# A kernel of two transformer blocks: the last attention pair's softmax rows over three PSUM banks, the low-rank weights loaded with the constants, and two more gate units in the first recurrence pair

## What is computed

```python
for g, (window, dilation) in enumerate(DILATED_GROUPS):
    num, den, mx = dilated_group_attention(...)
m_all = jnp.max(jnp.stack(maxes), axis=0)
wts = [jnp.exp(mx - m_all) for mx in maxes]
num_tot = sum(w[..., None] * n for w, n in zip(wts, nums))
den_tot = sum(w * d for w, d in zip(wts, dens))
o_attn = (num_tot / den_tot[..., None]).reshape(B, S, ATTN_WIDTH)
...
w_log = -jax.nn.softplus(-(rwkv_w0[l] + jnp.tanh(w_low) @ rwkv_w_up[l])) - 0.5
decay = jnp.exp(-jnp.exp(w_log))
a = jax.nn.sigmoid(rwkv_a0[l] + a_low @ rwkv_a_up[l])
...
y = rwkv7_scan(r4, decay.reshape(hs), k4, v4, -kk, kk * a.reshape(hs))
...
merged = jax.nn.sigmoid(g_attn) * y_attn + jax.nn.sigmoid(g_rwkv) * y_rwkv
```

## Time and profile before

| | |
|---|---|
| median of 3 runs | 2949.07 us (2947.56 to 2949.91) |
| the profiled execution | 2949.86 us, of which the traced span is 2948.1 us |
| mean granted PE clock | 0.961 |
| PE busy | 2738.0 us, 93% of the span |
| DVE busy | 1342.5 us, 46% |
| ACT busy, POOL busy | 815.2 and 818.1 us, 28% each |

### The profile page before, as it was taken

One profiled execution on the slowest core, in us unless ns is written; L12 is line 12 of the kernel. 1 busy time (PEld: TensorE's weight loads), 2 busy tenths in 40 slices (PEclk: granted clock), 3 DMA queues, 4 the chain that ended last, 5 costly groups with the idle time before them and its releaser, 6 DMA issues.

```text
span 2948.1 us, 43284 instructions
## 1 busy us (share of the span) xinstructions
PE 2738.0 (93%) x17944; PEld 2184.3 (74%) x17944; DVE 1342.5 (46%) x2316; ACT 815.2 (28%) x1584; POOL 818.1 (28%) x453
## 2 busy tenths in 40 slices
PE   6999999987979999999898999999998989999896
PEld 5787878775757667576677888788886877777675
DVE  4225252527647465474541433544444023677703
ACT  2444444443113131220212211211113013344432
POOL 2222222212112121220244132222332445333253
PEclk9999999998989999999999999999999989999887
DMA  3111111111001011011331211111111131111021
GB/s 120 40 45 39 57 33 58 36 41 47 23 15 58 16 47 34 26 51 52 143 118 58 79 43 51 36 50 43 43 43 43 43 121 65 29 30 29 29 86 57
DMA packets 204739, 153.42 MB, mean 52 GB/s; under 512 B 4864, under 2 KB 191616, under 8 KB 203776
## 3 DMA queue, kind: packets, MB, share of 16 engines
q1 hardware_dynamic: 191248, 102.25, 11.9%
q10 hardware_dynamic: 13296, 48.41, 4.2%
HBM read 127.57 MB, written 23.07 MB: 51 GB/s over the span
## 4 chain that ended last, share of the span: by engine, by line
PE 76%; DVE 16%; ACT 5%; issue 1%; DMA 1%; ACTq 0%; POOL 0%; DVEq 0%; SPq 0%; POOLq 0%
PE gemm L497 21%; PE gemm L499 19%; PE gemm L498 19%; ACT prob L1858 2%; DVE neg_logits L1413 2%; PE scores L728 1%; DVE prob L1428 1%; PE scores L548 1%; PE scores L739 1%; PE weighted L575 1%; PE probs_t L736 1%; PE probs_t L560 1%; PE scores L874 1%; PE weighted L799 1%; DVE alibi_tile L1443 1%
## 5 line engine op out<-in xcount | busy, mean ns | idle before, releaser
L497 PE MATMUL gemm<-h_hi,w_hi 128*128 128x512 f32 x1936 | 803.5, 415 | 9.7 <-ACT q_t L1617 7.6
L499 PE MATMUL gemm<-h_hi,w_lo 128*128 128x512 f32 x1936 | 762.0, 394 | 0.0
L498 PE MATMUL gemm<-h_lo,w_hi 128*128 128x512 f32 x1936 | 760.8, 393 | 0.0
L457 POOL CAST w_hi<-w_raw 128x1024 fp32r<-128x1024 f32 (+1 forms) x189 | 196.7, 1041 | 2026.0 <-PE gemm L499 2011.9
L458 POOL TENSOR_TENSOR w_lo<-w_raw,w_hi 128x1024 fp32r<-128x1024 f32 (+1 forms) x189 | 459.1, 2429 | 15.1
L497 PEld LDWEIGHTS gemm<-h_hi,w_hi 128*128 128x128 f32 x1936 | 366.9, 190 | 103.9 <-issue 23.1
L499 PEld LDWEIGHTS gemm<-h_hi,w_lo 128*128 128x128 f32 x1936 | 366.7, 189 | 80.2
L498 PEld LDWEIGHTS gemm<-h_lo,w_hi 128*128 128x128 f32 x1936 | 367.7, 190 | 65.2 <-issue 1.9
L1307 DVE TENSOR_TENSOR scaled_product<-gemm,norm_rstd 128x512 f32<-128x512 f32 x116 | 80.2, 692 | 336.8 <-PE gemm L499 330.2
L1293 DVE TENSOR_SCALAR stats<-weighted 128x8 f32<-128x8 f32 x5 | 0.8, 168 | 352.9 <-PE weighted L799 352.9
L1031 DVE CUSTOM_DVE_ANT_0 neg_logits<-scores,bias_tile 128x128 f32<-128x128 f32 (+1 forms) x192 | 67.7, 352 | 150.1 <-PE scores L548 144.3
(11 more groups left out here) (338 smaller groups left out, 4318.5 us busy)
## 6 DMA issues: line engine op xcount, KB each, us to landing
w_raw<-in_w_in SPq DMA_DIRECT2D x73, 512.0 KB, 3.9
w_raw<-in_a_w_in SPq DMA_DIRECT2D x48, 512.0 KB, 3.7
gates_scratch<-o_f ACTq DMA_DIRECT2D x32, 256.0 KB, 2.0
merge_gates<-gates_scratch ACTq DMA_DIRECT2D x4, 2048.0 KB, 15.1
w_raw<-in_a_w_out SPq DMA_DIRECT2D x16, 512.0 KB, 3.3
w_raw<-in_b_w_in SPq DMA_DIRECT2D x16, 512.0 KB, 3.8
x_rows<-in_x SPq DMA_DIRECT2D x8, 512.0 KB, 8.6
w_raw<-in_w_out SPq DMA_DIRECT2D x8, 512.0 KB, 3.4
```

The source lines that it names most:

```text
L457: Q(pool.tensor_copy(whi[:, s, 0:nk, :], raw[:, s, 0:nk, :]))
L497: pe.matmul(G[b][:], whi[:, s, k, :], hi(k, h), start=first, stop=False)
L498: pe.matmul(G[b][:], whi[:, s, k, :], lo(k, h), start=False, stop=False)
L499: m = pe.matmul(G[b][:], wlo[:, s, k, :], hi(k, h), start=False, stop=last)
```

## The change

Six things change. (1) For the last pair, the sets j = 0, 1 and 2 of the stat rows are transposed in slot 83 into three different banks, `MB` and the two halves of `S2` (`scores`), and set 3 in slot 84 into `MB` again. PE then waits for the last scores to be read, for the three earlier pairs' copies, and, for set 3 alone, for ACT's first copy of this pair. (2) `row_den` moves to 105.75 KB, and ACT issues both loads of `lora_up` right behind the constants. (3) `GATES_BEFORE` gives pair 0 four gate units in place of two, pair 1 three in place of four, pair 2 four as before, and pair 3 five in place of six. (4) Pair 0 gets 24 steps at `in` (8 before) and 12 at `norm` (4 before). Ten of the 24 stand ahead of the first spreading of weights, six between the spreadings, eight behind. (5) The clearing of the last pair's weights goes ahead of `best_of`. (6) DVE waits for the three earlier pairs' output to be stored before it blends the last.

The pairs then have 128, 112, 128 and 96 steps, and the scans get 30, 28, 44 and 12 of them.

```diff
-GATES_BEFORE, SIDE_PRE, SIDE_IN, SIDE_NORM, SIDE_BONUS, SIDE_AMAT, SIDE_ROWS, SIDE_INV = (0, 2, 6, 10, 16), (3, 2, 3, 2), 8, 4, 20, (2, 2, 2, 3), (3, 2, 2, 2, 2), 11 * (1, 1)
+GATES_BEFORE, FIRST_IN, FIRST_NORM, SIDE_PRE, SIDE_IN, SIDE_NORM, SIDE_BONUS, SIDE_AMAT, SIDE_ROWS, SIDE_INV = (0, 4, 7, 11, 16), 24, 12, (3, 2, 3, 2), 8, 4, 20, (2, 2, 2, 3), (3, 2, 2, 2, 2), 11 * (1, 1)
 FAR = 1e30
...
         st_max = at("row_max", 124, [P, 8, 66])
-        st_den = at("row_den", 204, [P, 8, 66])
+        st_den = at("row_den", 105.75, [P, 8, 66])
         pick_raw = at("pick_raw", 102, [P, 2 * P])
...
             counts = {f"pre{f}": SIDE_PRE[f] * (p > 0) for f in range(4)}
-            counts.update({"in": SIDE_IN, "norm": SIDE_NORM, "bonus": SIDE_BONUS})
+            counts.update({"in": SIDE_IN if p else FIRST_IN, "norm": SIDE_NORM if p else FIRST_NORM, "bonus": SIDE_BONUS})
             counts.update({f"amat{f}": SIDE_AMAT[f] for f in range(4)})
...
         stat_slots = {20 * p + 23 + j: [(p, j)] for p in range(LAST) for j in range(4)}
-        stat_slots.update({20 * LAST + 23: [(LAST, 0), (LAST, 1)], 20 * LAST + 24: [(LAST, 2), (LAST, 3)]})
+        stat_slots.update({20 * LAST + 23: [(LAST, 0), (LAST, 1), (LAST, 2)], 20 * LAST + 24: [(LAST, 3)]})
+
+        def stat_bank(p, j):
+            return (MB[:], S2[:, 0:HALF], S2[:, HALF:], MB[:])[j if p == LAST else 0]
+
         best_slots = {20 * p + (27 if p < LAST else 25): p for p in range(PAIRS)}
...
                     pe.wait_ge(E("blended"), 6 * p)
-                if 4 * p + j > 0:
+                if p == LAST:
+                    pe.wait_ge(E("ttr_done"), len(quads))
+                    pe.wait_ge(E("stat_in"), 4 * p + (j == 3))
+                elif 4 * p + j > 0:
                     pe.wait_ge(E("stat_in"), 4 * p + j)
                 for i in range(4):
-                    m = pe.transpose(MB[0:66, i * P:i * P + P], (st_max, st_den)[j // 2][:, 4 * (j % 2) + i, :], ident)
+                    m = pe.transpose(stat_bank(p, j)[0:66, i * P:i * P + P], (st_max, st_den)[j // 2][:, 4 * (j % 2) + i, :], ident)
                 m.then_inc(E("stat_tr"), 1)
...
                 if p == 0:
+                    for e in range(10):
+                        gemm_step(U_SIDE[0], e // 8, e % 8, *H1)
                     for b in range(6):
                         spread_weight(LAST, b)
-                        gemm_step(U_SIDE[0], 0, b, *H1)
-                    for b in range(6, 8):
-                        gemm_step(U_SIDE[0], 0, b, *H1)
+                        gemm_step(U_SIDE[0], 1, 2 + b, *H1)
+                    for e in range(16, FIRST_IN):
+                        gemm_step(U_SIDE[0] + e // 16, e // 8 % 2, e % 8, *H1)
                     pe.wait_ge(E("blended"), 6 * PAIRS)
...
                 if s in best_slots:
+                    if best_slots[s] == LAST:
+                        V(v.memset(weight[LAST][:].bitcast(F32), 0.0))
                     best_of(best_slots[s])
...
                 if s in weight_slots:
-                    if weight_slots[s] == LAST:
-                        V(v.memset(weight[LAST][:].bitcast(F32), 0.0))
                     weight_of(weight_slots[s])
...
             mixed_in(3)
+            dve.wait_ge(E("oa_out"), 16 * LAST)
             for b in range(6):
...
             act.dma_start(pick_raw[:], d["shape_consts"][:, NCONST:NCONST + 2 * P]).then_inc(E("pick_in"), 16)
+            act.dma_start(upw[0:64, :], d["rwkv_w_up"][0]).then_inc(E("up_in"), 16)
+            act.dma_start(upw[64:128, :], d["rwkv_a_up"][0]).then_inc(E("up_in"), 16)
...
                 hn, dst = j % 2, (rw_max, rw_den)[j // 2]
-                A(a.activation(dst[32 * hn:32 * hn + 2, 0, :], MB[0:2, :], ACT.Copy))
-                src1 = MB[32:34, :].rearrange("p (r x q) -> p x r q", r=2, x=2)
-                src2 = MB[64:66, :].rearrange("p (r x l) -> p x r l", r=8, x=2)
+                rows = stat_bank(p, j)
+                A(a.activation(dst[32 * hn:32 * hn + 2, 0, :], rows[0:2, :], ACT.Copy))
+                src1 = rows[32:34, :].rearrange("p (r x q) -> p x r q", r=2, x=2)
+                src2 = rows[64:66, :].rearrange("p (r x l) -> p x r l", r=8, x=2)
                 for th in range(2):
...
-            act.dma_start(upw[0:64, :], d["rwkv_w_up"][0]).then_inc(E("up_in"), 16)
-            act.dma_start(upw[64:128, :], d["rwkv_a_up"][0]).then_inc(E("up_in"), 16)
             lo_, hi_ = slice(0, 64), slice(64, 128)
...
             def side_out(p, place):
```

## The result

The changed kernel took 2938.43 us (median of 8 runs, 2930.34 to 2940.76), the kernel before 2949.71 us (8 runs beside them). The ratio is 0.9948, with an interval of 0.9934 to 0.9963. Two later comparisons gave 0.9953 (0.9940 to 0.9966) and 0.9934 (0.9917 to 0.9951). So the change is worth 11 to 20 us, where 22.9 were forecast: the sign was right, the size too large.

What follows compares the result with a forecast made beforehand. PE, busy 93% of the span, was taken as the bound, so only its waits and lower clock could yield. Terms −14.9 − 1.4 − 0.8 − 2.9 − 2.9 = −22.9 us from 2949.07 gave 2926.2 us, range 2919 to 2934.

Steps and rivals of the forecast that it cites:

- The stat rows: End of the attention loop: both waits for ACT's copies go, so PE is done 13.4 us earlier, at 665.0.
- rival (a): Slots 83 to 87: ACT becomes the bound or the low part comes late; some 5 us come back, 2931.2; chance 0.12.
- The low-rank weights: After attention: the 10.3 us wait for `lora_up` goes; products end at 666.9, then 0.9 us wait for the v half's bank.
- the low part's chain: Ahead of the first spread: the weights' low part ends at 672 or by 670.2, so PE does not wait.
- The ten steps: Side steps ahead of the first spreading of weights: they take 6.9 us, to 674.7.
- The spreading, the norms, the products: First spread at 674.7, norms' spread at 699.3 without wait, 14.9 us earlier; then 1.4 and 0.8 us less before the products.
- the inverse head: Head of the inverse: PE's waits of 1.5 and 1.4 us for DVE beside POOL's addition go, 2.9 us.
- The scans: Scans of pairs 0, 1 and 3: moved side steps, collisions with POOL and the clock sum to −2.9 us.
- leaving the scan at that clock: End of pair 1's scan, last two chunks unfilled: the lower clock costs 0 to 2.7 us, taken as +1.2.
- Rival (b): Scans: three whole POOL blocks, not one, +5, and lower clock behind, +2; 2933.2; sign: distances above 4.5 us; chance 0.10.
- rival (c): Setup: the new loads hold up `pick`, giving 2930; sign: PE's first wait for `q_t` above 8.5 us; chance 0.04.
- Rival (e): After pair 3's scan: lower clock stays through recurrence's end and merge, 2956; sign: half clock behind 1420 us; chance 0.03.

Runs made afterwards that it cites:

- stats_only: Kernel before with only the last pair's stat rows put through three banks; 2944.73 us, ratio 0.9961.
- again_after: Changed kernel run again with no edit, beside the kernel before; ratio 0.9953.
- v_half_first: Changed kernel with the `lora_up` loads issued in slot 20 and ACT copying the first v half before writing the weights' high part; 2932.84 us, ratio 0.9944.
- up_only: Kernel before with only the low-rank weights loaded early, in slot 20 of the attention loop; 2951.03 us, ratio 0.9985.
- stats_and_up: Kernel before with the three banks and the low-rank weights loaded in slot 20, side steps as before; 2939.97 us, ratio 0.9949.
- thick_all: v_half_first with the scans of pairs 0, 1 and 3 filled three steps to a chunk from the front; 2931.09 us, ratio 0.9914.
- again_before: Kernel before run again with no edit; ratio to the kernel before 1.0004.
- warm_more: v_half_first with 32 unused matmuls added around the first late norm; 2930.82 us, ratio 0.9923.
- fill_waits: v_half_first with side steps before the norms' spread raised from 4 to 7 (pairs 1 to 3), before the products from 20 to 22; 2942.59 us, ratio 0.9965.

## Why the prediction was too low

**The stat rows: right.** 13.4 us were counted and 13.4 measured, by stats_only and by the low-rank products at 664.9 us in again_after (counted: 665.0). ACT kept its margins; rival (a)'s wait in slots 84 to 87 did not come.

**The low-rank weights: the wait right, what is late next too small.** The 10.3 us went. The wait for the v half's bank was counted at 0.9 us and is 2.3. The copy is queued behind the high part, which was put at 666.4 and ended at 669.6; the profile was 2.0 us late at slot 82, so 1.2 us of that are the prediction's. The step that failed is the one that put the low part's chain at its earliest end, 670.2: it ended at 673.8, or 671.8 with the 2.0 us off, 1.6 us later than that and at the 672 that stood beside it. The low part came before PE wanted it, as taken.

**The ten steps: the price was taken at the full clock.** 6.9 us were counted and they took 8.5, at 0.80 behind that wait. The prediction charged the clock behind every wait that it removed and not behind the one that it left. V_half_first, without the wait, has the full clock. These two make 3.0 us.

**The spreading, the norms, the products: right.** From the first spread to the spread of the norms 24.6 us were counted, 24.4 to 25.0 measured. PE's spread after the norms is at the full clock, where the earlier trace rows had 3.36 us:

```profile
704.66 1.97 PE L639 MATMUL scores<-consts_sb,stats 128*64 128x128 f32 x32 [0.57 <-DVE stats L1168]
```

The next stage to the products takes 19.0 us (counted 19.0), and that to the scan 73.6 us (73.8 counted): the 2.9 us of the inverse head are there.

**The scans: the mean about right for pairs 0 and 3, pair 1 and the untouched pair 2 wrong.** Pair 0 took 63.5 to 64.1 us (counted 63.3), pair 3 51.6 to 52.0 (52.6). Pair 1 was counted at 62.6 and took 62.9, 64.9 and 64.5. The failed step is where the sum charges the lower clock: once, for leaving the scan ("leaving the scan at that clock costs 0 to 2.7 us", taken at +1.2), and not behind a collision. There each chunk at half clock costs 2.0 us (5.3 for 3.33), one of them in the first profile and two in the others. The clock is at half in the last chunks too, but that is paid only where it outlasts the scan: from the end of pair 1's scan to pair 2's products it is 44.0, 44.0 and 46.4 us, where before has 45.2. Pair 2, counted at nothing, took 66.1 us in all three profiles for 64.7 before, a 5.2 us chunk behind its collision. Its code and steps are the same; up_only and stats_and_up show the extra time too, stats_only, thick_all and v_half_first do not. In the first profile 1.7 us more were lost from the products to the scan of pair 3 (75.3 us for 73.6), behind a fall of the clock at 1269.5 us. Rival (b) named the right place and put it at 7 us; in the scans of pairs 1 and 2 it is 2 to 4. Its sign, distances above 4.5 us at more than two places, told nothing: pair 1 has three and four of them now, and had four before.

**The setup: rival (c) was partly right.** Two loads behind `pick` on the same queue delayed it by 0.6 us, where (c) had 3.8, and PE's first wait stayed below its sign of 8.5 us. The rule on ring order that the prediction set against this (the Trainium skill, DMA: Bandwidth & Descriptors, "Queues, rings and completion order") speaks of the order in which one queue's descriptors are taken. What these rows show is that keeping one's place in the queue does not keep one's time.

**Behind the recurrence: not a term at all.** I took the difference from two single executions as if the untouched 1500 us were constant. Again_before shows 7.6 us between two runs of one kernel there. In the first comparison the changed kernel's profile lost 1.3 us up to the late norm, 4.2 at it and 1.5 at the end; in again_after it lost nothing, and its span is 17.8 us ahead. Rival (e) did not come: the clock is back at its full level 1.0 to 2.2 us into the merge, in before 2.2 us. The first profile does have half clock behind 1420 us, the sign of (e), but for 3.4 us and once.

So of the 22.9 us, 3.0 were lost at the spreading, 0 to 2 ahead of slot 82, of which the setup's loads explain 0.6, and 1.6 to 4.1 in the recurrence. That leaves 15 to 17 us at its end, as measured (16.1, 17.4, 15.5); what is behind that is the run's. Why one chip has before at 2949 and another at 2957 was not settled, nor what decides whether the lower clock stays for one chunk or three.

## What to carry to other kernels

Charge the lower clock behind each wait that a change leaves, not only behind those that it removes, and look for the copy that is queued behind an operation which itself waits: turning two of ACT's operations round was worth 3.9 us at the spreading. Side work in a scan is more than filler. In pair 1, with three steps to a chunk, one chunk behind the collision with GpSimd ran partly at the lower clock (1.4 us); with two it was one to three chunks at up to 2.0 us each, so the price of taking a step out is read from the chunks that collide, not from the quiet ones. And before a difference of 1% is predicted from one profile, it pays to have a second profile of the same kernel: what differs between the two is no part of the sum.

## What the runs showed of the hardware

- The granted clock of TensorE stays at half for different lengths behind the same wait in the same code: in again_after 13 us passed from the wait's end to the full clock, in again_before about 25. In pair 1's scan it is one chunk (5.3 us) in one profile and three (16 us) in another.
- At half clock it is not only long matmuls that take longer: the sixteen one-column matmuls of a norm sum took 3.41 to 3.58 us there and 1.84 at the full clock (again_after).
- Dense unused matmuls carried the full clock through what had been a wait of 6.5 us (warm_more), and it fell nonetheless at 1605.9 us, among the norm sums and behind a wait of 1.0 us.
- Two DMA issues behind another one on ACT's queue, 128 KB each, delayed its landing by 0.6 us, from some 4.8 to some 5.4 us after its issue.
- DVE's operations of 128 x 1024 took 3.27 and 3.26 us beside POOL's split and addition in fill_waits, where one outside them took 1.22 in v_half_first. POOL's took 3.23 and 3.21 us there, and 2.37 and 2.35 in v_half_first, although DVE's operation beside the second of these (930.89 us) took 3.27: not each overlap makes both longer.
